# Router logits from unnormalised residual chunks, and modulated rows made by GpSimd and ScalarE, in a four-layer float32 model on one core

## The chip, the core and the metric

The kernel runs on one core of one Trainium2 chip. The metric is the device time of one execution in microseconds (us); less is better. A profiled execution lists every instruction of the five engines: TensorE (PE, and PEld for its weight loads), VectorE (DVE), ScalarE (ACT), GpSimd (POOL) and SyncE (SP, whose DMA queue is SPq), with the names of the tiles that it writes and reads.

## What is computed

Two blocks of two layers each, 512 tokens of width 1024, all float32. The first block has an attention layer and a state-space layer, each followed by a hierarchical mixture of experts (MoE) with 32 experts of which each token takes two. The second block has two layers with a context of 256 tokens beside the 512. The change touches the way into the two MoE layers:

```python
x = x + gate1[:, None, :] * mix
h2 = modulate(rmsnorm(x, norm2_w[layer]), shift2, scale2)   # h * (1 + scale) + shift
# hier_moe(h2, ...), t = h2 by tokens:
g_prob = softmax(t @ w_group + b_group);  g_val, g_idx = top_k(g_prob, 1)
e_logits = einsum('td,dge->tge', t, w_expert) + b_expert     # those of group g_idx
e_val, e_idx = top_k(softmax(e_logits), 2);  e_val = e_val / sum(e_val)
hid = silu(t @ w1[e]) * (t @ w3[e]);  y = sum over the two e of weight * (hid @ w2[e])
```

## The kernel before

Each engine has its own program, written out by hand; the order in the file is the order in which the engine works, and semaphores join them. Activations lie transposed: `xT` and `hT` hold 8 slices of 128 channels by 512 tokens (`hT` has 256 context columns behind them). Weights stream through `ring`, eight slots of 128x8x128 (512 KB each), filled by SyncE in the order of use: a slot is requested again when the product that used it is done (`put`, L1526). A product takes eight matmuls of 128 rows each into one of eight PSUM banks; banks go round in the order of the `job(...)` calls, and a job waits until its bank's last user has been copied out (L691 to L717). A float32 matmul is two instructions in the profile.

The stretch in question comes twice, as layer 0 and layer 1 of the first block:

1. The last product of the mixer gives the residual in eight parts (`outA` for layer 0, `out_part`, job `outM`, for layer 1). VectorE adds each to `xT` (`residual`, L2498; L2885 and following for layer 1), ScalarE squares it (`squares`), VectorE adds up the squares (`sum_square`, L2486).
2. Between these products TensorE has parts of the adaptive modulation: a "quad" is four blocks of modulation columns, computed in four parts of four ring slots (`quad_part`, L803), copied by ScalarE (`quad_out`), turned by `quad_turn` (L818) and added to the bias by VectorE (`quad_add`). Quads 4 and 8 are spread over the routing.
3. `norm_sum` (L828) sums the squares over channels with one product, ScalarE takes the root (`inv_root`: Ln, then Exp, into `rstd`).
4. `modulated` (L2324) on VectorE: for each slice `hT = xT * A * rstd` and then `+ shift`, 16 operations.
5. `moe(l)` on TensorE (L880): the route product of `rw` (36 columns: 4 groups and 32 experts) with the eight slices of `hT`; transposes of `hT` to rows of tokens (`token_rows`, jobs `h_tok`), which ScalarE copies and stores to `h_dram` (four stores of 512 KB); then small products that serve VectorE's chain.
6. `route(l)` on VectorE (L2509): logits with bias, group and expert maxima with masks, "picks", prefix sum over tokens, block and lane of each pair, and at its end the token numbers `pair_u`. Most are operations on 128x16 to 128x200.
7. GpSimd gathers rows of `h_dram` by `pair_u` with indirect DMAs once all rows are stored (`h_rows_stored`), TensorE transposes them (`rows_T`, L961), and the expert steps follow (`up`, L976; `down`, L995).

In layer 1 TensorE also works off three columns of the next block's context product in this stretch (`first_ctx`, `ctx_column`, L876), each 3.6 us, cut in halves between the small products; ScalarE copies them into `ctx_kept`.

GpSimd does nothing else in the stretch. In the state-space stage it forms sums of weights for halved products (`pair_sums`, L3379), four tensor_tensor of 128x512 a pair.

## Time and profile before

| | us |
|---|---|
| median of 3 runs | 3356.8 |
| lowest, highest | 3356.3, 3364.9 |
| profiled execution, its own time | 3363.0 |
| its span, from the first to the last instruction | 3361.0 |

| engine | busy us | share of the span |
|---|---|---|
| TensorE, matmuls | 3218.6 | 96% |
| TensorE, weight loads | 2058.4 | 61% |
| VectorE | 1757.3 | 52% |
| ScalarE | 883.7 | 26% |
| GpSimd | 285.8 | 9% |

The mean granted TensorE clock is 0.982 of full speed, the DMA moved 399 MB. In a timeline each row is a run of like instructions: its start, its length, engine, line of the file, operation, what it writes and reads, how many; in brackets how long the engine was idle before it, and what ended that. The last residual product of layer 0 ends at 294.8 us from the span's start, that of layer 1 at 1056.2.

### The profile page before, as it was taken

How to read it: one execution, taken by the hardware profiler on the slowest of the kernel's cores; microseconds unless marked ns; L12 is line 12 of the kernel's file. 1: busy time of each engine (PE TensorE's matmuls, PEld its weight loads, DVE VectorE, ACT ScalarE, POOL GpSimd, SP SyncE). 2: the span in 40 equal slices, each digit the busy share in tenths (PEclk: the TensorE clock that was granted, in tenths of full speed). 3: DMA queues.
4: the chain of work that ended last, by engine and by line, in shares of the span. 5: the costliest groups of instructions: out<-in, count | busy, mean ns of one | idle time of the engine just before them, and what ended most of it. 6: DMA issues, size and time to landing. Idle time of an engine off the chain costs nothing.

```text
span 3361.0 us, 36905 instructions
## 1 busy us (share of the span) xinstructions
PE 3218.6 (96%) x13516; PEld 2058.4 (61%) x13516; DVE 1757.3 (52%) x3507; ACT 883.7 (26%) x1775; POOL 285.8 (9%) x246
## 2 busy tenths in 40 slices
PE   7988998999999999999999999999999999999998
PEld 4743653777744655565555555555544666878887
DVE  2253235787724236986344454444468854454555
ACT  2241221334321221154232131111111623222212
POOL 1200431243200330000000000000000000000000
PEclk9999999999999899999999999999999999999999
DMA  8646877533247786111111112222222111223232
GB/s 269 215 157 224 312 293 242 161 106 98 82 167 262 288 319 174 31 32 55 38 38 50 51 49 64 57 57 57 58 69 69 37 51 50 76 69 88 82 88 63
DMA packets 427392, 399.00 MB, mean 119 GB/s; under 512 B 28080, under 2 KB 362416, under 8 KB 419792
## 3 DMA queue, kind: packets, MB, share of 16 engines
q1 hardware_dynamic: 393520, 352.60, 33.3%
q10 hardware_dynamic: 15264, 24.07, 2.2%
q0 software_dynamic: 18432, 19.98, 1.8%
q8 instruction: 111, 1.82, 0.2%
q14 instruction: 65, 0.53, 0.1%
HBM read 445.37 MB, written 31.92 MB: 142 GB/s over the span
## 4 chain that ended last, share of the span: by engine, by line
PE 60%; DVE 7%; DMA 2%; issue 1%; ACT 1%; POOL 0%; SPq 0%; DVEq 0%; ACTq 0%; POOLq 0%
PE psum L751 39%; PE psum L736 5%; PE psum L1279 3%; DVE arena L2240 3%; PE psum L976 3%; DMA ring<-in_w_branch 1%; PE psum L995 1%; PE psum L1441 1%; PE psum L1453 1%; PE psum L1365 1%; PE psum L1405 1%; PE psum L1395 1%; DVE arena L2237 1%; PE psum L961 1%; ACT scratch L1662 1%
## 5 line engine op out<-in xcount | busy, mean ns | idle before, releaser
L751 PE MATMUL psum<-arena,ring 128*128 128x384 f32 (+1 forms) x2592 | 747.2, 439 | 13.1 <-DVE psum L2237 6.1
L751 PEld LDWEIGHTS psum<-arena,ring 128*128 128x128 f32 x2592 | 491.9, 191 | 239.8 <-DVE psum L2237 13.3
L751 PE MATMUL psum<-hT,ring 128*128 128x384 f32 (+1 forms) x2176 | 622.1, 439 | 0.0
L751 PEld LDWEIGHTS psum<-hT,ring 128*128 128x128 f32 x2176 | 413.7, 190 | 187.4 <-issue 5.7
L1670 ACT ACTIVATE scratch<-psum 128x256 f32<-128x256 f32 (+1 forms) x411 | 176.2, 429 | 962.4 <-PE psum L751 814.6
L2237 DVE TENSOR_TENSOR ring<-ring 128x512 f32<-128x512 f32 (+1 forms) x336 | 216.1, 662 | 261.8 <-PE psum L751 250.2
L2237 DVE TENSOR_TENSOR psum<-psum,scratch 128x256 f32<-128x256 f32 (+1 forms) x328 | 155.8, 480 | 371.3 <-PE psum L751 270.0
L1670 ACT ACTIVATE arena<-psum 128x512 f32<-128x512 f32 (+5 forms) x414 | 194.2, 500 | 470.3 <-PE psum L736 139.9
L736 PE MATMUL psum<-hT,ring 128*128 128x512 f32 (+1 forms) x704 | 282.5, 562 | 6.0 <-DVE hT L2233 6.0
L1662 ACT ACTIVATE arena<-psum,cols 128x256 f32<-128x256 f32 (+3 forms) x280 | 131.7, 493 | 521.7 <-PE psum L976 228.4
L2240 DVE SCALAR_TENSOR_TENSOR arena<-arena,vec 128x783 f32<-128x783 f32 (+1 forms) x256 | 228.7, 894 | 9.1
L736 PEld LDWEIGHTS psum<-hT,ring 128*128 128x128 f32 x704 | 134.7, 192 | 151.7 <-issue 142.5
L2237 DVE TENSOR_TENSOR arena<-arena 128x512 f32<-128x512 f32 (+13 forms) x252 | 186.3, 753 | 45.4 <-DMA arena<-y_dram 20.9
L2240 DVE SCALAR_TENSOR_TENSOR arena<-arena,psum 128x384 f32<-128x384 f32 (+3 forms) x236 | 98.3, 448 | 206.1 <-ACT arena L1662 195.6
L1064 PE MATMUL psum<-hT,ring 128*128 128x256 f32 x672 | 154.4, 381 | 0.0
L1662 ACT ACTIVATE arena<-arena,cols 128x512 f32<-128x512 f32 (+10 forms) x171 | 137.1, 830 | 54.6 <-DVE arena L2240 24.5
L1064 PEld LDWEIGHTS psum<-hT,ring 128*128 128x128 f32 x672 | 126.4, 190 | 19.8 <-issue 3.4
L2237 DVE TENSOR_TENSOR arena<-psum,scratch 128x384 f32<-128x384 f32 (+1 forms) x80 | 40.8, 510 | 157.1 <-PE psum L751 157.1
L751 PE MATMUL psum<-arena,scratch 128*128 128x384 f32 (+1 forms) x384 | 113.9, 432 | 3.8 <-DVE arena L2237 3.8
L1279 PE MATMUL psum<-arena,ring 128*128 128x512 f32 x256 | 111.8, 595 | 0.9 <-DVE hT L2240 0.9
L976 PE MATMUL psum<-arena 128*64 128x256 f32 x960 | 111.3, 386 | 1.4 <-issue 1.4
L1064 PE MATMUL psum<-arena 128*128 128x256 f32 x448 | 101.3, 379 | 0.0
(269 smaller groups left out, 3605.2 us busy)
## 6 DMA issues: line engine op xcount, KB each, us to landing
ring<-in_w_in SPq DMA_DIRECT2D x177, 512.0 KB, 4.0
arena<-in_moe_w SPq DMA_DIRECT2D x44, 1536.0 KB, 10.9
ring<-in_ada_w SPq DMA_DIRECT2D x96, 512.0 KB, 5.9
ring<-in_w_mod SPq DMA_DIRECT2D x48, 512.0 KB, 5.9
ring<-in_ssm_w_in SPq DMA_DIRECT2D x48, 512.0 KB, 5.5
ring<-in_w_branch SPq DMA_DIRECT2D x64, 256.0 KB, 3.2
hT<-in_moe_w SPq DMA_DIRECT2D x10, 1536.0 KB
ring<-in_moe_w SPq DMA_DIRECT2D x10, 1024.0 KB
```

Source lines behind the costliest of these rows:

```text
L736: mm = nc.tensor.matmul(b[:, 0:n], ws[k // 8][0][:, k % 8, :], rhs(k)[:, o:o + n], start=(k == 0), stop=(k == nk - 1))
L751: mm = nc.tensor.matmul(flat(bank_, nb), lhs[:, k, :], rhs(k), start=(start and k == 0), stop=(k == kd_ - 1), skip_group_check=True)
L961: mm = nc.tensor.transpose(b[:, j * P:(j + 1) * P], rows[:, i % DEEP, k * P:(k + 1) * P], C("ident"))
L976: mm = nc.tensor.matmul(b[LANES * h:LANES * h + LANES, 0:2 * P], rowsT[:, i % 2, k, LANES * h:LANES * h + LANES], step_weights(s, h, 2 * P ...
L995: mm = nc.tensor.matmul(b[LANES * h:LANES * h + LANES, :], hidT[:, i % 2, LANES * h:LANES * h + LANES], step_weights(s, h, w0, S), start=T ...
L1064: mm = nc.tensor.matmul(bank_[:, 0:S // 2], lhs[:, k, :], rhs(k), start=(start and k == 0), stop=(k == 3), skip_group_check=True)
L1279: mm = nc.tensor.matmul(b, ws[k // 8][0][:, k % 8, :], yT[:, k, :], start=(k == 0), stop=(k == 15))
L1365: mm = nc.tensor.matmul(b[:, 0:w], z_w[c][0][:, k, :], hT[:, k, o:o + w], start=(k == 0), stop=(k == KD - 1))
L1662: return nc.scalar.activation(out_, in_, f, bias=bias, scale=scale, **kw)
L1670: return nc.scalar.activation(out_, in_, ACT.Copy)
L2237: return v.tensor_tensor(out_, in0, in1, op)
L2240: return v.scalar_tensor_tensor(out_, in0, s, in1, op0, op1)
```

## The change

Route logits. With A = norm2_w * (1 + scale) the route product of the modulated rows is the root of a token times the product of `rw` with `xT * A`, plus the product of `rw` with the shift. So:

- VectorE writes `hT = xT * A` for each slice as soon as the slice's residual is there (`scaled`), and no longer runs `modulated` ahead of the routing.
- TensorE runs the route product on these: slices 0 to 5 ahead of the last residual product (layer 0) or in its middle (layer 1), slice 6 and slice 7 behind it, on either side of the norm sum (`route_part`). Eight one-column products give the shift's part of the logits (`route_shift`), which VectorE adds to the router's bias.
- VectorE multiplies the product by the root and adds the bias, two operations instead of one.
- GpSimd multiplies the eight slices of `hT` by the root, in place, once the route product has read them; ScalarE adds the shift. Both run beside VectorE's routing chain.
- Token rows are transposed by halves (channels 0 to 511 of all tokens, then the rest), placed among the small products; ScalarE stores each half by itself, eight stores of 256 KB.
- Parts 2 and 3 of quads 4 and 8 come behind the logits' transposes. In layer 1 the context columns are no longer cut in halves, quad 5 moves one residual product earlier, and its turn ahead of the last one; the context's modulation on VectorE moves from c = 6 to c = 5.

```diff
+            def route_part(l, k0, k1):
+                if k0 == 0:
+                    eng.wait_ge(rw_landed, pe.at(("rw", l)))
+                    b, full = job("route_shift", l)
+                    eng.wait_ge(vector_done, pe.at(("quad", (1, 4)[l])))
+                    for k in range(KD):
+                        mm = nc.tensor.matmul(b[0:36, 0:1], rw[:, k, :], col("mod", 48 * l + 24 + k), start=(k == 0), stop=(k == KD - 1))
...
+                for k in range(k0, k1):
+                    eng.wait_ge(vector_done, pe.at(("scaled", l, k)))
+                    mm = nc.tensor.matmul(b[0:36, :], rw[:, k, :], hT[:, k, 0:S], start=(k == 0), stop=(k == KD - 1))
...
             def moe(l):
+                route_part(l, KD - 2, KD - 1)
+                quad_part(QUAD_MOE[l], 0)
+                norm_sum(f"n2_{l}")
+                route_part(l, KD - 1, KD)
                 quad_part(QUAD_MOE[l], 1)
...
@@ TensorE, layer 0
                 linear(("outA", c), lambda k: aT[:, k, :])
                 if c == 6:
                     quad_turn(3)
+                    if stage_on(2):
+                        route_part(0, 0, KD - 2)
...
@@ TensorE, layer 1
-                    if c >= 4:
-                        quad_part(5, c - 4)
-                    out_part(c, 0, 16)
+                    if c < 7:
+                        quad_part(5, c - 3)
+                        out_part(c, 0, 16)
                 quad_turn(5)
+                out_part(7, 0, 8)
+                if stage_on(4):
+                    route_part(1, 0, KD - 2)
+                out_part(7, 8, 16)
...
@@ ScalarE, moe
+                for half in range(2):
+                    for k in range(4 * half, 4 * half + 4):
+                        eng.wait_ge(gpsimd_done, ac.at(("rooted", l, k)))
+                        act(hT[:, k, 0:S], hT[:, k, 0:S], ACT.Identity, bias=col("mod", 48 * l + 24 + k)).then_inc(scalar_done, ac.step(("h", f"n2_{l}", k)))
+                    if half == 0:
+                        quad_out(QUAD_MOE[l])
+                for half in range(2):
+                    for t in range(4):
                         evac(("h_tok", l, t, half), h_tok[:, t, half * S:(half + 1) * S])
-                    if t == 0:
-                        quad_out(QUAD_MOE[l])
-                    eng.wait_ge(scalar_done, ac.own())
-                    eng.dma_start(h_dram[l][t * P:(t + 1) * P, :], h_tok[:, t, :]).then_inc(h_rows_stored, 16)
+                        eng.wait_ge(scalar_done, ac.own())
+                        eng.dma_start(h_dram[l][t * P:(t + 1) * P, half * S:(half + 1) * S], h_tok[:, t, half * S:(half + 1) * S]).then_inc(h_rows_stored, 16)
+                    if l and half == 0:
+                        evac(("att_k", 0, 0, "c"), ctx_kept[:, 0:L], n=L, name=("ctx_kept", 0))
...
@@ VectorE
+            def scaled(l, k):
+                eng.wait_ge(vector_done, ve.own())
+                ts(hT[:, k, 0:S], xT[:, k, :], col("A", k)).then_inc(vector_done, ve.step(("scaled", l, k)))
...
             def route(l):
+                eng.wait_ge(rb_landed, ve.at(("rb", l)))
+                b, free = full("route_shift", l)
+                tt(rb[0:36, :], rb[0:36, :], b[0:36, 0:1], ALU.add).then_inc(vector_done, ve.step(free))
                 b, free = full("route", l)
-                eng.wait_ge(rb_landed, ve.at(("rb", l)))
-                ts(logitT[0:36, :], b[0:36, :], rb[0:36, :], op0=ALU.add).then_inc(vector_done, ve.step([free, ("biased", l)]))
+                eng.wait_ge(scalar_done, ve.at(("rstd", f"n2_{l}", "x")))
+                tt(logitT[0:36, :], b[0:36, :], rstd[0:36, 0:S], ALU.mult).then_inc(vector_done, ve.step([free, ("rstd_used", f"n2_{l}")]))
+                eng.wait_ge(vector_done, ve.own())
+                ts(logitT[0:36, :], logitT[0:36, :], rb[0:36, :], op0=ALU.add).then_inc(vector_done, ve.step(("biased", l)))
...
-                modulated("n2_0", V("norm2_w", 0, 8), M(0, 4, 0, 8), lambda k: M(0, 3, k), lambda k: xT[:, k, :])
...
@@ GpSimd, moe
-                eng.wait_ge(h_rows_stored, 64 * (l + 1))
+                eng.wait_ge(tensor_done, po.at(("full",) + jobname("route", l)))
+                eng.wait_ge(scalar_done, po.at(("rstd", f"n2_{l}", "x")))
+                for k in range(KD):
+                    g_.tensor_tensor(hT[:, k, 0:S], hT[:, k, 0:S], rstd[:, 0:S], ALU.mult).then_inc(gpsimd_done, po.step(("rooted", l, k)))
+                eng.wait_ge(h_rows_stored, 128 * (l + 1))
```

TensorE around the last residual product of layer 0 (L736), up to the second weight part of quad 4, in the order before. L814 is a weight part, L834 the norm sum, L886 the route product.

```order
L736 MATMUL psum<-arena,ring 128x512 x7
L814 MATMUL psum<-ring,arena 32x512 [waits weights_1,weights_2,weights_0,weights_3,vector_done]
L814 MATMUL psum<-ring,arena 32x512 x7
L834 MATMUL psum<-scratch,ones 128x512 [waits vector_done]
L814 MATMUL psum<-ring,arena 32x512 [waits weights_6,weights_7,weights_5,weights_4]
L814 MATMUL psum<-ring,arena 32x512 x7
L886 MATMUL psum<-hT,arena 36x512 [waits vector_done,rw]
L886 MATMUL psum<-hT,arena 36x512 [waits vector_done] x7
```

The same place in the order now; L889 is the shift's product, L895 the route product, L918 the logits' transposes.

```order
L889 MATMUL psum<-cols,arena 36x1 x7
L895 MATMUL psum<-hT,arena 36x512 [waits vector_done] x6
L736 MATMUL psum<-arena,ring 128x512 [waits vector_done,weights_7]
L736 MATMUL psum<-arena,ring 128x512 x7
L895 MATMUL psum<-hT,arena 36x512 [waits vector_done]
L814 MATMUL psum<-ring,arena 32x512 [waits weights_1,weights_2,weights_0,weights_3,vector_done]
L814 MATMUL psum<-ring,arena 32x512 x7
L834 MATMUL psum<-scratch,ones 128x512 [waits vector_done]
L895 MATMUL psum<-hT,arena 36x512 [waits vector_done]
L814 MATMUL psum<-ring,arena 32x512 [waits weights_6,weights_7,weights_5,weights_4]
L814 MATMUL psum<-ring,arena 32x512 x7
L918 MATMUL psum<-const,arena 128x36 [waits vector_done]
```

Six slices of the route product and the shift's product have moved ahead of the last residual product; one slice stands on each side of the norm sum, and the logits' transposes follow the second weight part.

TensorE in layer 1, from the third context column to the row transposes, before. L876 is a context column; of the small products that serve VectorE's chain L938 is for the experts, L944 for the pairs, L951 for the weights of the slots; L961 are the row transposes.

```order
L876 MATMUL psum<-hT,arena 128x256 [waits scalar_done,vector_done,ctx_w]
L876 MATMUL psum<-hT,arena 128x256 x3
L938 MATMUL psum<-arena,ones 128x16 [waits vector_done,scalar_done]
L944 MATMUL psum<-arena 128x24 [waits vector_done,scalar_done]
L944 MATMUL psum<-arena 128x24 x7
L876 MATMUL psum<-hT,arena 128x256 x4
L951 MATMUL psum<-arena 128x24 [waits vector_done]
L951 MATMUL psum<-arena 128x24 x7
L961 MATMUL psum<-const,arena 128x128 [waits scalar_done,rows_0]
```

The same place now, from the last token rows (L912) and the turn (L824) on; L957 is for the experts, L963 for the pairs, L970 for the weights of the slots, and the row transposes follow.

```order
L912 MATMUL psum<-const,hT 128x128 [waits scalar_done] x8
L824 MATMUL psum<-const,arena 128x8 [waits scalar_done]
L824 MATMUL psum<-const,arena 128x8 x3
L876 MATMUL psum<-hT,arena 128x256 [waits scalar_done,vector_done,ctx_w]
L876 MATMUL psum<-hT,arena 128x256 x7
L957 MATMUL psum<-arena,ones 128x16 [waits vector_done]
L963 MATMUL psum<-arena 128x24 [waits vector_done,scalar_done]
L963 MATMUL psum<-arena 128x24 x7
L876 MATMUL psum<-hT,arena 128x256 [waits scalar_done,vector_done,ctx_w]
L876 MATMUL psum<-hT,arena 128x256 x7
L970 MATMUL psum<-arena 128x24 [waits vector_done]
L970 MATMUL psum<-arena 128x24 x7
```

Token rows stand among the small products, and two whole context columns stand between the turn and the weights of the slots, where two halves of one column stood.

## Rows read from the trace of the kernel before

**Rows 1.** Busy time by stretch (us, engines' busy us and instructions, clock, DMA).
```profile
296.00:345.00 49.00, 34.12 (x180) 20.47 (x174) 26.78 (x94) 10.43 (x19) 6.12 (x6) 0.77 0.64 225
1056.00:1106.00 50.00, 45.73 (x240) 28.62 (x239) 27.93 (x96) 11.20 (x20) 6.02 (x6) 0.88 0.71 248
```
**Rows 2.** TensorE's timeline, layer 0, 270 to 350 us.
```profile
287.68 7.11 PE L736 MATMUL psum<-arena,ring 128*128 128x512 f32 x16
294.72 1.92 PE L814 MATMUL psum<-ring,arena 128*32 128x512 f32 x16
297.32 1.10 PE L834 MATMUL psum<-scratch,ones 128*128 128x512 f32 x2 [0.67 <-DVE cols L2237]
...
302.02 8.16 PE L886 MATMUL psum<-hT,arena 128*36 128x512 f32 x16 [1.55 <-DVE hT L2233]
...
314.71 0.44 PE L902 MATMUL psum<-const,arena 36*128 36x36 f32 x4
...
321.81 0.60 PE L919 MATMUL psum<-const,arena 128*32 128x128 f32 x4 [3.90 <-DVE arena L2237]
...
341.15 3.65 PE L961 MATMUL psum<-const,arena 128*128 128x128 f32 x16
```
**Rows 3.** TensorE's timeline, layer 1, 1000 to 1125 us.
```profile
1042.38 13.97 PE L1279 MATMUL psum<-arena,ring 128*128 128x512 f32 x32 [0.86 <-DVE hT L2240]
1056.19 0.95 PE L824 MATMUL psum<-const,arena 128*128 128x4 f32 x8
...
1061.72 1.92 PE L814 MATMUL psum<-ring,arena 128*32 128x512 f32 x16 [1.68 <-DMA ring<-in_w_mod]
...
1072.77 3.64 PE L814 MATMUL psum<-ring,arena 128*32 128x512 f32 x32
...
1079.38 3.62 PE L876 MATMUL psum<-hT,arena 128*128 128x256 f32 x16
...
1095.58 3.76 PE L876 MATMUL psum<-hT,arena 128*128 128x256 f32 x8
...
1102.41 1.95 PE L961 MATMUL psum<-const,arena 128*128 128x128 f32 x8
```
**Rows 4.** VectorE's timeline, layer 0, 270 to 350 us.
```profile
315.18 0.31 DVE L2515 COPY arena<-psum 128x144 f32<-128x144 f32 x1 [4.22 <-PE psum L902]
...
317.30 0.78 DVE L2243 TENSOR_REDUCE arena<-arena 128x8 f32<-128x32 f32 x5
...
321.71 0.48 DVE L2570 MEMSET arena<- 32x512 f32 x1
...
335.84 0.18 DVE L2623 CAST pair_u<-arena 128x24 uint32<-128x24 f32 x1
```
**Rows 5.** VectorE's timeline in the state-space stage, 640 to 690 us.
```profile
660.92 0.42 DVE L2237 TENSOR_TENSOR psum<-psum,scratch 128x256 f32<-128x256 f32 x1
...
680.72 1.38 DVE L2237 TENSOR_TENSOR arena<-arena,hT 128x512 f32<-128x512 f32 x1
```
**Rows 6.** GpSimd's timeline in the same stretch.
```profile
660.85 1.27 POOL L3394 TENSOR_TENSOR arena<-ring,arena 128x512 f32<-128x512 f32 x1
...
680.29 1.27 POOL L3392 TENSOR_TENSOR arena<-arena,ring 128x512 f32<-128x512 f32 x1
```
**Rows 7.** ScalarE's timeline, layer 0, 270 to 350 us.
```profile
299.24 0.72 ACT L1662 ACTIVATE scratch<-scratch,cols 128x512 f32<-128x512 f32 x1
...
317.44 1.08 ACT L1670 ACTIVATE arena<-psum 128x512 f32<-128x512 f32 x2 [0.42 <-PE psum L893]
...
318.93 1.09 ACT L1670 ACTIVATE arena<-psum 128x512 f32<-128x512 f32 x2 [0.40 <-ACT arena L1670]
```
**Rows 8.** TensorE by stretch: us, busy, clock, DMA share, GB/s; layer 1.
```profile
1064.00:1068.00 4.00, 3.97 (x9) 1.00 1.02 367
```
**Rows 9.** The same view, two stretches of one us in layer 0.
```profile
322.00:323.00 1.00, 0.41 (x4) 0.71 1.01 408
346.00:347.00 1.00, 1.00 (x10) 0.84 1.02 430
```

More of the change, by code:

```diff
@@ L903, in moe @@
                 mm.then_inc(tensor_done, pe.step(full))
-                for t in range(1, 4):
-                    token_rows(t)
+                quad_part(QUAD_MOE[l], 2)
+                quad_part(QUAD_MOE[l], 3)
                 def first_ctx(i, k0, k1):
@@ L2889, in _ @@
                     if c == 6:
+                        quad_add(5)
+                        eng.wait_ge(vector_done, ve.own())
+                        stt(col("A", 0, 8), M(1, 4, 0, 8), 1.0, V("norm2_w", 8, 8), ALU.add, ALU.mult).then_inc(vector_done, ve.step())
+                        for k in range(KD - 1):
+                            scaled(1, k)
+                    if c == 7:
+                        scaled(1, 7)
+                    if c == 5:
                         stt(col("A2", 0, 8), col("mod2", 32, 8), 1.0, V("norm_w_2", 0, 8), ALU.add, ALU.mult).then_inc(vector_done, ve.step())
```

66 lines of the change are left out of this document (30 added, 36 removed).

## The prediction

> **What bounds the kernel now.** I read the busy time by stage first. TensorE is busy for 96% of the span, and the two routing stages are among the few places where it is not: 34.1 of 49 us in the first mixture-of-experts layer (layer 0), 45.7 of 50 us in the second (layer 1) [rows 1]. Second, TensorE's timeline in both. In layer 0 the last residual product ends at 294.8 and the first transposes of gathered rows start at 341.15, so routing takes 46.3 us; TensorE waits 1.55 us for the modulated rows, 3.9 us for the picks, and several times behind them [rows 2]. In layer 1 the same stretch runs from 1056.2 (where the turn that follows that product starts) to 1102.4, 46.2 us, but context columns fill it, such as the one that starts at 1079.38, and the waits sum to about 4 us (50.0 less 45.7, [rows 1]), 1.68 of it a wait for streamed weights [rows 3]. Third, VectorE's timeline: a chain of short operations on 128 partitions, logits copied at 315.18, picks done when the memset of 321.71 starts (6.5 us), token numbers cast at 335.84, which frees the gathers [rows 4]. What bounds layer 0 is that chain; layer 1 is bound by TensorE's own work almost as much as by the chain.
>
> **The change, part by part.** I call the end of the last residual product T before and T' after, and count from it.
>
> *Ahead of T'.* Six of eight slices of the route product now run ahead of the last residual product (layer 0) or in its middle (layer 1). A 512-column product of one slice costs 7.1/8 = 0.89 us [rows 2], so 5.3 us. They were in the routing stretch before, where the eight took 8.2 us, paced by VectorE. New are eight one-column products for the shift. Where the trace has none like them, the nearest are those of the turn: narrow instructions cost 0.95/8 = 0.12 us each however narrow [rows 3]; at two instructions a product that is 1.9 us at most; at nothing, 0. I take 1.7. TensorE has no idle time ahead of T, so nothing covers this: T' is 7.0 us later than T. In layer 1 the turn (0.95) also moves ahead of T', and the wait of 0.86 us at the last residual product [rows 3] should go, since that product's weights are now requested earlier: 7.1 us.
>
> *The root off the chain.* After T' come slice seven 0.9, the first weight part 1.9, the norm sum 1.1, slice eight 0.9: the route product is full at 4.8. The root is ready 1.5 us after the norm sum (which ends at 298.4 [rows 2], the Exp at 299.96 [rows 7]), at 5.4. The multiply by the root takes 0.75, like the biased copy before, then the new bias add 0.4, the logits' transposes 0.45 [rows 2]: logits copied at about 8, where it was 20.35 before (315.18 less 294.83). VectorE's 16 operations of modulation leave this path, and the two weight parts (2 and 3) that stood ahead of the logits' transposes now stand behind. That is a lead of 12 us for the chain. The eight added scaling operations hide under TensorE's 7 us products; were they late, slices one to six would be.
>
> *GpSimd beside the chain.* Eight products 128x512 of two SBUF inputs start at 5.5 and take 1.27 each, as GpSimd's weight sums do [rows 6]. That is where the lead is spent. The trace shows it in the state-space stage. GpSimd's product at 680.29 ends at 681.56; VectorE's two-input operation of 512 columns that started at 680.72 took 1.38 and ended at 682.10, half a microsecond after GpSimd's, so most of what it took was waiting. The tensor_tensor at 660.92, which reads PSUM and one SBUF tile, took 0.42 beside GpSimd's product of 660.85 and waited for nothing [rows 5, 6]. So a two-input operation of VectorE waits for the GpSimd product under way to end. Of the routing chain nearly every tensor_tensor has two SBUF inputs; the reductions and the PSUM reads have one. While GpSimd has products left, the chain gets about one such operation per 1.3 to 1.4 us. GpSimd is done at 5.5 + 8 x 1.27 + 8 x 0.2 for VectorE's turns = 17.3. By then about ten operations of the chain are through (bias add, group maximum, group pick, the four masks) and what starts at 317.30 in the old trace (4.4 us to the picks [rows 4]) is left: picks at 21.7. If the four masks pass together it is 20.5. I take 21.6. Before, it was 26.9. The rule of the Trainium skill, page "SBUF — State Buffer", section "Who interferes with whom", says the same: a VectorE instruction with two SBUF inputs contends with a GpSimd instruction that reads SBUF, and whoever is second fully blocks. It speaks against this change, and the row at 680.72 agrees. By it the picks come at 21.6; with no such hold they would come at 14.4, which is rival A.
>
> *Streamed weights.* After T' ten transfers of 512 KB are still to come (two of part 1, parts 2 and 3), since a ring of eight slots can only be refilled as it is used. The DMA moved 367 GB/s there [rows 8]: 5.24 MB in 14.3 us plus a microsecond to start. Part 3 lands at 15 and is used by 17. Before, parts 2 and 3 were used at 16.5 and later (1072.77, [rows 3]) and never waited; now TensorE reaches them at 8 and waits 2.1 and 3.7 us. In layer 0 that hides behind the chain (17 against 21.6).
>
> *Layer 0 after the picks.* The chain behind the picks is as it was, 19.4 us to the row transposes with its waits (321.71 to 341.15 [rows 2, 4]); TensorE has the token transposes between the steps now, at the half clock, which costs 0.6. Row transposes at 21.6 + 19.4 + 0.6 = 41.6 instead of 46.3: -4.7, with +7.0 ahead of T': **+2.3 us**.
>
> *Layer 1 after the picks.* TensorE has more to do here: eight token groups (3.8 us), ctx column 1 and 2 whole (3.6 each [rows 3]). The second-half token transpose needs the bank of context column 0, which ScalarE empties only behind four copies and four stores of the first half; two copies and a store take 1.5 us (317.44 to 318.93 [rows 7]), so a copy and a store 1.05 by estimate, and so that bank is free at 27. Slots go at 28 instead of 27, the pair product starts at 34.2 (the chain alone would have it 1.5 us earlier), gathers are issued at 38.5, and TensorE is through column 2 and the weight product between 43.5 (full clock) and 47.7 (half clock; the eight slices at 1095.58 took 3.76 at it [rows 3]). I take 45.3 against 46.2: -0.9, with +7.1: **+6.2 us**.
>
> Expert loads start when part 3 is used, 3 us later than before against a first use 22 us on; nothing there. The last row store goes out at about 30 (31 in layer 1), 3 us to land, and token numbers come at 36 (38); were the copies 3 us later, this store would end the wait. The sum is 2.3 + 6.2 = 8.5 us. The profiled execution took 3363.0 (span 3361.0), the median of the runs is 3356.8; I put the sum on the median: **3365 us**, 0.25% slower, inside what a measurement of this kernel can tell from no change (0.3%, 10 us).
>
> **Rivals.**
> *A, VectorE is not held.* For it: no row shows operations of 0.17 us beside GpSimd; four masks without waits may slip through together with their followers. Against: [rows 5, 6]. Picks at 14.4; TensorE ends part 3 at 17 and is next: picks transposed at 17.1 in layer 0 (26.98 before), -9.9 + 7.0 = -2.9; in layer 1 column 0 ends at 20.9, 0.7 earlier than in my forecast, +5.5. Sum +2.6, 3359.
> *B, the clock holds and faster.* The granted clock fell to half between 322 and 323 in layer 0, behind the wait for the picks, and came back between 346 and 347 [rows 9]. With fewer idle microseconds it could stay up. The column slices of 1095.58 would take 1.8 instead of 3.76, the sixteen transposes of 341.15 half of their 3.65 [rows 2, 3], and their neighbours likewise: by estimate 4 us in each layer. On top of A: -6, 3351. Against: the sparse stretch behind the picks is still there.
> *C, an early clock fall, slower.* The idle time before the picks was 3.9 us when the clock fell [rows 2, 9]. Now TensorE is busy 1.9 of the 7.2 us from 7.8 to 15 while it waits for weights. If the clock falls there, part 3 costs 3.8 instead of 1.9 and column 0 up to 7.2 instead of 3.6, until the clock comes back (dense work ran from 341.15 at the latest to past 346 before it did [rows 2, 9], by estimate 5 to 9 us): in layer 1 the picks are transposed at 25.3, not 21.7, +3.7; together +12 to +13, 3370. In layer 0 the chain hides it. It decides if the fall comes before 16.
> *D, the change does not do what it says*: the logits come no earlier, because slice eight or the root is late. Both have producers that were there before; 2%, inside the range.
>
> **How the numbers follow.** Forecast 0.50 (+3 to +12), A 0.22 (0 to +5), B 0.08 (-10 to -3), C 0.18 (+9 to +18), D 0.02. The range takes B's near half to C's upper end: 3351 to 3375. Faster by over 0.3% needs both layers at their best: 0.05. Slower by over 0.3% is three quarters of C and a quarter of the forecast: 0.26. Same: 0.69.
>
> **What would show it.** Right: T' 7 us later; logits copied near 8; two-input operations of VectorE of 1 to 1.4 us between them and GpSimd's last product; waits of TensorE for weights ahead of parts 2 and 3; picks at 20 to 22; the row transposes of layer 1 no earlier than 43 after T'. Wrong: VectorE's chain still at 6.5 us beside GpSimd; shift products of next to nothing; a gain of over 5 us in layer 1, which would mean that its idle time was larger than its 4 us, or that its clock stayed up.

## The result, and the profile after it

| | before | changed |
|---|---|---|
| median of 6 runs (lowest to highest) | 3357.8 us (3355.1 to 3364.9) | 3375.2 us (3371.0 to 3378.2) |
| profiled execution: time, span | 3363.0, 3361.0 | 3375.5, 3373.6 |

The ratio is 1.0044, 95% interval 1.0033 to 1.0054: slower by 0.44%, some 15 us. The forecast was 3365 (3351 to 3375). The measured median lies at the upper edge of the range, 0.2 us past it; the ratio, put on the median of 3356.8 that the forecast started from, gives 3371.6, inside it. The prediction gave 0.69 to a change of at most 0.3% and 0.26 to a loss of more than that, and it was the loss.

Busy time by stretch in the changed kernel (columns as in [rows 1]; the first two answer to those rows, the third is in the attention stage of the first layer, ahead of all that was changed):

```profile
304.00:349.00 45.00, 30.33 (x169) 18.08 (x168) 26.45 (x80) 15.10 (x24) 14.30 (x13) 0.72 0.68 230
1075.00:1125.00 50.00, 38.07 (x219) 23.62 (x219) 26.52 (x81) 16.74 (x28) 16.08 (x14) 0.83 0.72 245
168.00:190.00 22.00, 17.05 (x54) 9.89 (x54) 14.54 (x41) 8.90 (x28) 0.00 (x0) 0.62 0.62 224
```

TensorE is busy for 38.1 us of layer 1's routing stretch, where it was 45.7 of as many. The third row explains a part of the difference that is not the change's: the granted clock in 168 to 190 us was 0.62, in the profiled execution of before 0.84, and the last residual product of layer 0 ended 9.8 us later, of which the inserted work is only 5.9. So I compare stretches from T', not times of day.

TensorE's timeline of the changed kernel, layer 0 (answers to [rows 2]; columns: start us, duration us, engine, line, operation, output<-inputs, shapes, count, idle time before it and what ended it):

```profile
290.81 0.95 PE L824 MATMUL psum<-const,arena 128*128 128x4 f32 x8
291.70 0.72 PE L889 MATMUL psum<-cols,arena 128*36 128x1 f32 x16
292.28 5.32 PE L895 MATMUL psum<-hT,arena 128*36 128x512 f32 x12
297.53 7.13 PE L736 MATMUL psum<-arena,ring 128*128 128x512 f32 x16
304.59 1.05 PE L895 MATMUL psum<-hT,arena 128*36 128x512 f32 x2
...
312.19 0.41 PE L918 MATMUL psum<-const,arena 36*128 36x36 f32 x4 [0.55 <-DVE arena L2260]
315.60 2.74 PE L814 MATMUL psum<-ring,arena 128*32 128x512 f32 x16 [3.00 <-DMA ring<-in_ada_w]
321.51 3.64 PE L814 MATMUL psum<-ring,arena 128*32 128x512 f32 x16 [3.17 <-DMA ring<-in_ada_w]
...
325.99 1.01 PE L937 MATMUL psum<-const,arena 128*32 128x128 f32 x4
...
347.09 3.25 PE L980 MATMUL psum<-const,arena 128*128 128x128 f32 x14 [1.41 <-DMA arena<-h_dram,pair_u]
```

T' is 304.6. The insert takes 5.9 us: from the start of the turn (290.81) to the start of the last residual product (297.53) it is 6.7 us, before it was 0.8 (286.87 to 287.68). Part 2 waits 3.00 and part 3 3.17 us for their weights; part 3 ends at 325.1, 20.5 after T'. Rows are transposed 42.5 after T' (before: 46.4 after T).

VectorE and GpSimd beside it (the routing chain, answers to [rows 4]):

```profile
312.63 0.31 DVE L2552 COPY arena<-psum 128x144 f32<-128x144 f32 x1 [0.59 <-PE psum L918]
312.98 0.17 DVE L2270 TENSOR_REDUCE arena<-arena 128x4 f32<-128x16 f32 x1
313.18 1.26 DVE L2264 TENSOR_TENSOR arena<-arena 128x16 f32<-128x16 f32 x1
314.47 1.19 DVE L2260 TENSOR_SCALAR arena<-arena 128x16 f32<-128x16 f32 x1
315.69 1.22 DVE L2264 TENSOR_TENSOR arena<-arena,const 128x16 f32<-128x16 f32 x1
316.94 0.17 DVE L2270 TENSOR_REDUCE arena<-arena 128x4 f32<-128x16 f32 x1
317.15 3.65 DVE L2264 TENSOR_TENSOR arena<-arena 128x16 f32<-128x16 f32 x5
...
325.23 0.48 DVE L2607 MEMSET arena<- 32x512 f32 x1
```
```profile
310.49 10.05 POOL L3404 TENSOR_TENSOR hT<-hT,scratch 128x512 f32<-128x512 f32 x8 [161.82 <-ACT scratch L1683]
343.54 1.19 POOL L3377 DMA_INDIRECT arena<-h_dram,pair_u  x1 [22.99 <-DMA h_dram<-arena]
```

The logits are copied 8.0 after T'. Until GpSimd is done at 320.5, operations of 0.17 us with tiles in SBUF take 1.2 (reductions excepted), and the five of 317.15, of which the first is the group mask, 3.65 (0.71 before). The picks are there at 325.2, 20.6 after T', after a chain of 12.6 us (6.5 before). The gather of 343.54 was ended by the row stores, not by the token numbers (cast at 340.2).

Layer 1, first its weights at the third output product, some 90 us ahead of T', where the change multiplies quad 5 one product earlier; then the head of the routing (answers to [rows 3]):

```profile
970.41 11.32 PE L1298 MATMUL psum<-arena,ring 128*128 128x512 f32 x26
983.88 1.92 PE L814 MATMUL psum<-ring,arena 128*32 128x512 f32 x16 [2.15 <-DMA ring<-in_ada_w]
988.11 15.67 PE L1298 MATMUL psum<-arena,ring 128*128 128x512 f32 x32 [2.31 <-DMA ring<-in_ssm_w_out]
```
```profile
1068.11 7.13 PE L1298 MATMUL psum<-arena,ring 128*128 128x512 f32 x16
1075.17 1.05 PE L895 MATMUL psum<-hT,arena 128*36 128x512 f32 x2
...
1082.78 0.41 PE L918 MATMUL psum<-const,arena 36*128 36x36 f32 x4 [0.33 <-DVE arena L2260]
1086.64 3.64 PE L814 MATMUL psum<-ring,arena 128*32 128x512 f32 x16 [3.46 <-DMA ring<-in_w_mod]
1092.70 3.64 PE L814 MATMUL psum<-ring,arena 128*32 128x512 f32 x16 [2.42 <-DMA ring<-in_w_mod]
1096.27 4.67 PE L876 MATMUL psum<-hT,arena 128*128 128x256 f32 x16
1100.78 0.60 PE L937 MATMUL psum<-const,arena 128*32 128x128 f32 x4
```

And the granted clock (the last column but two) in stretches of it:

```profile
1080.00:1084.00 4.00, 2.70 (x21) 0.82 (x20) 2.27 (x5) 1.83 (x4) 2.93 (x3) 1.00 1.01 367
1084.00:1088.00 4.00, 1.36 (x8) 0.45 (x12) 3.86 (x5) 1.96 (x3) 4.00 (x4) 0.57 1.02 361
1092.00:1096.00 4.00, 3.30 (x16) 0.68 (x16) 3.54 (x22) 0.00 (x0) 0.00 (x0) 0.50 0.00 1
1100.00:1120.00 20.00, 17.60 (x121) 15.56 (x119) 9.80 (x36) 6.31 (x13) 2.68 (x3) 1.00 0.69 240
```

T' is 1075.2. TensorE idled 3.5 us from 1083.2 on, the clock went to its lower level (0.50), and parts 2 and 3 took 3.64 each instead of 1.9. The picks were transposed 25.6 after T', though they had been made at 20.6.

### The profile page after: what moved, and what is told of

It reads as the page before. It is cut to its first block, busy times and chain, and to the rows that moved or that the text cites. A ratio compares the mean times of both kernels' runs of the same rounds, so it can differ in the third digit from the quotient of the medians.

```text
span 3373.6 us, 37016 instructions
## 1 busy us (share of the span) xinstructions
PE 3221.9 (96%) x13548; PEld 2056.5 (61%) x13548; DVE 1763.1 (52%) x3495; ACT 895.3 (27%) x1791; POOL 305.5 (9%) x262
## 4 chain that ended last, share of the span: by engine, by line
PE 81%; DVE 7%; DMA 3%; ACT 2%; issue 2%; ACTq 0%; POOL 0%; SPq 0%; DVEq 0%; POOLq 0%
PE psum L751 39%; PE psum L1083 7%; PE psum L736 7%; PE psum L995 5%; PE psum L1298 3%; DVE arena L2267 3%; PE psum L1014 3%; DMA ring<-in_w_branch 1%; PE psum L980 1%; PE psum L1462 1%; PE psum L1474 1%; PE psum L1261 1%; PE psum L814 1%; PE psum L1386 1%; PE psum L843 1%
## 5 line engine op out<-in xcount | busy, mean ns | idle before, releaser
L736 PE MATMUL psum<-hT,ring 128*128 128x512 f32 (+1 forms) x704 | 281.1, 559 | 5.8 <-DVE hT L2260 5.8
L736 PEld LDWEIGHTS psum<-hT,ring 128*128 128x128 f32 x704 | 134.2, 192 | 150.9 <-issue 142.1
L2264 DVE TENSOR_TENSOR arena<-arena 128x512 f32<-128x512 f32 (+13 forms) x252 | 195.5, 790 | 44.9 <-DMA arena<-y_dram 20.4
L2264 DVE TENSOR_TENSOR arena<-psum,scratch 128x384 f32<-128x384 f32 (+2 forms) x82 | 42.2, 514 | 163.1 <-PE psum L751 157.4
L2267 DVE SCALAR_TENSOR_TENSOR xT<-psum,cols,xT 128x512 f32<-128x512 f32 (+1 forms) x64 | 37.7, 613 | 122.5 <-PE psum L736 62.2
```

Of the source, the lines that this page charges most:

```text
L736: mm = nc.tensor.matmul(b[:, 0:n], ws[k // 8][0][:, k % 8, :], rhs(k)[:, o:o + n], start=(k == 0), stop=(k == nk - 1))
L2264: return v.tensor_tensor(out_, in0, in1, op)
L2267: return v.scalar_tensor_tensor(out_, in0, s, in1, op0, op1)
```

## The experiments

Twelve kernels in four batches (numbers 1 to 4, 5 to 8, 9 and 10, 11 and 12); each batch with runs of the kernel before beside it (medians 3361.2, 3360.5, 3360.6 and 3359.0 us).

**1. Quad 5 alone.** Before, with only quad 5 multiplied and loaded one product earlier:

```diff
-                    if c >= 4:
-                        quad_part(5, c - 4)
+                    if c < 7:
+                        quad_part(5, c - 3)
```

> The kernel before with one thing of the change only: quad 5 is read and multiplied one residual product earlier (c = 3 to 6 instead of 4 to 7), its turn and its bias stay where they were. Theory (the stall is in the prefetch): in the changed kernel TensorE waits 2.15 us for the first weight part of quad 5 and 2.31 us for the residual product behind it, and that product takes 15.7 instead of 14.0 us, 6.1 us in all, and the 0.86 us wait at the last residual product is gone; so +4 to +6 us. Rival (the stall belongs to the new order of DMAs and banks elsewhere in the changed kernel): +0 to +1 us.

Measured: 3365.1, ratio 1.0012 (1.0003 to 1.0021).

```profile
966.53 11.32 PE L1279 MATMUL psum<-arena,ring 128*128 128x512 f32 x26
979.98 2.81 PE L814 MATMUL psum<-ring,arena 128*32 128x512 f32 x16 [2.13 <-DMA ring<-in_ada_w]
984.28 15.67 PE L1279 MATMUL psum<-arena,ring 128*128 128x512 f32 x32 [1.50 <-DMA ring<-in_ssm_w_out]
```

Before, TensorE goes through here without a wait. From the code I read it so: products 0 to 2 keep their slots until their last slices are multiplied together, and four more loads of 512 KB come into an interval in which hardly a slot is free. The 0.86 us wait that the move removes costs two waits of 3.6 us together, a part at 2.81 instead of 1.92 and a product at 15.67 instead of 14.00. From the first of these products to T it is 97.8 us, 5.4 more than before.

**2 and 3. The change in one layer.** In layer 0 alone (the layer 1 code as before, quad 5 too), and in layer 1 alone with quad 5:

```diff
-                route_part(l, KD - 2, KD - 1)
-                ...
+                if l in NEW:
+                    route_part(l, KD - 2, KD - 1)
+                    ...
+                else:
+                    ...
```

> The change in layer 0 only; layer 1 as before, quad 5 too. Theory (the sum of the terms of the prediction, with the shift's products at 0.7): T' 6.0 later, 42.4 from T' to the row transposes instead of 46.3: +2 us. Rival (GpSimd's hold costs more than the lead in each layer): +5 or more. Other rival (layer 0 gains by itself, the whole loss is in layer 1): -3 or less.

> The change in layer 1 only, with quad 5 one product earlier; layer 0 as before. Theory: +6 to +7 from slices, shift and turn ahead of T' with nothing gained behind it (45.8 instead of 46.2 us to the row transposes), and +5 from the prefetch stall: +11 to +13 us. Rival (clock falls and noise of the attention stage make up a third of the measured +17): +7 or less.

Measured: layer 0 alone 3362.5, ratio 1.0002 (0.9991 to 1.0013); layer 1 alone 3376.6, ratio 1.0039 (1.0024 to 1.0054). Together they make 1.0041 of the 1.0044. The loss is layer 1's: about 13 us, of which quad 5 alone is 4.

**4. GpSimd's products cut to one column.** The change, with the hold on VectorE taken away by making its cause small:

```diff
-  g_.tensor_tensor(hT[:, k, 0:S], hT[:, k, 0:S], rstd[:, 0:S], ALU.mult)
+  g_.tensor_tensor(hT[:, k, 0:1], hT[:, k, 0:1], rstd[:, 0:1], ALU.mult)
```

> The changed kernel with GpSimd's eight products cut to one column each, so the rows that the experts get are not multiplied by the root. Theory (VectorE waits for GpSimd's product under way): the chain from the copied logits to the picks goes from 12.6 us (312.63 to 325.23) back to 6.5 us in both layers; TensorE is then held by the weight parts 2 and 3, so the row transposes come 3 to 4 us earlier in layer 0 and 0 to 1 us in layer 1: 3 to 5 us less than the changed kernel, still +11 to +14 against before. Rival (the chain is slow for another reason, such as ScalarE or the semaphores of eight more steps): chain above 11 us, no gain.

Measured: 3375.5, ratio 1.0042 (1.0029 to 1.0056), the same as the change. The chain is back at 6.5 us (logits copied at 312.46, picks at 318.98), so the hold was real, 6.1 us in each layer. And it was worth nothing, where I had expected 3 to 5 us. TensorE, layer 0 of this kernel:

```profile
316.29 3.31 PE L814 MATMUL psum<-ring,arena 128*32 128x512 f32 x16 [3.86 <-DMA ring<-in_ada_w]
322.40 2.60 PE L814 MATMUL psum<-ring,arena 128*32 128x512 f32 x16 [2.80 <-DMA ring<-in_ada_w]
...
325.84 1.06 PE L937 MATMUL psum<-const,arena 128*32 128x128 f32 x4
```

Picks made at 319 are transposed at 325.8, behind part 3. In layer 1 they are transposed 22.5 after T' instead of 25.6, and yet the rows come at 46.2 (45.75 in the change).

**5. The slices behind T'.** The change with its insert taken away from before T' in both layers, quad 5 back in its place:

```diff
-                    if stage_on(2):
-                        route_part(0, 0, KD - 2)
...
-                route_part(l, KD - 2, KD - 1)
-                quad_part(QUAD_MOE[l], 0)
+                route_part(l, 0, 2)
                 norm_sum(f"n2_{l}")
-                route_part(l, KD - 1, KD)
-                quad_part(QUAD_MOE[l], 1)
+                route_part(l, 2, KD)
+                quad_part(QUAD_MOE[l], 0)
...
+                quad_part(QUAD_MOE[l], 1)
                 quad_part(QUAD_MOE[l], 2)
...
```

Part 1 now stands behind the logits' transposes. The turn of quad 5 stays in the middle of the last product.

> The changed kernel, with what it put ahead of the last residual T' taken away again: the shift product and slices 0 to 5 stand behind T' in both layers (order now: shift, slices 0 and 1, the norm's sum, slices 2 to 7, quad part 0, logits, parts 1 to 3), and layer 1's quad 5 is multiplied where it was before the change, only its turn stands in the middle of the last output product. GpSimd's products stay as they are. Theory (the change loses by what it puts on TensorE and on the weights' path ahead of T', 6.0 us in layer 0 and about 10 in layer 1, and gains less behind it): T' comes back to its place of before, the 2.1 and 2.3 us waits for quad 5's and the output weights go, logits are copied about 12.5 after T' instead of 8, picks at about 25 with the hold (12.6 us of chain), rows transposed about 43 to 44.5 after T' against 46.3 and 46.2 before: 2 to 3 us less than before the change in each layer, total 3352 to 3358 beside 3357 to 3361 before, against 3375 for the change. Rival (layer 1 loses by something else in its head, the clock fall or the ctx columns): T' of layer 1 comes back but the stretch behind it stays at 46 or more, total 3360 to 3366.

**6. The same with GpSimd's products split** around the picks, each also waiting for its own slice of the route product only:

```diff
-  eng.wait_ge(tensor_done, po.at(("full",) + jobname("route", l)))
   ...
   for k in range(KD):
+      if k == 4:
+          eng.wait_ge(vector_done, po.at(("picks", l)))
+      eng.wait_ge(tensor_done, po.at(("routed", l, k)))
```

> As the run with the slices behind T', and GpSimd's eight products are split: product k waits for route slice k and the root alone, so that 0 to 3 can start some 5 us before the route product ends, and 4 to 7 wait until the picks are made. Theory (the hold of 6 us on VectorE's two-input operations is real, and it was worth nothing in the changed kernel only because weight parts 2 and 3 stand ahead of the transposed picks there; with the slices behind T' the weights are in by 17 and used by about 21 and bind no more): chain of the routing from logits copied to picks back to about 6.5 us, picks about 19 to 20 after T', picks transposed at 21 to 22, rows transposed at 39 to 42, total 4 to 6 us per layer under the kernel before, 3347 to 3352. Rival 1 (the hold is worth nothing anywhere): the same time as the run with the slices behind T', within 2 us. Rival 2 (the row stores take over, since h 4 to 7 now come about 8 us later): the gather ends its wait by the row stores, and rows are transposed at 43 or later: no gain over the other run or a loss.

Measured: 3375.3, ratio 1.0041 (1.0027 to 1.0054), and 3371.9, ratio 1.0048 (1.0031 to 1.0065). Both theories of mine missed by 17 us and more. Number 6, layer 0:

```profile
304.14 1.92 PE L814 MATMUL psum<-ring,arena 128*32 128x512 f32 x16
306.00 0.43 PE L916 MATMUL psum<-const,arena 36*128 36x36 f32 x4
306.36 1.92 PE L814 MATMUL psum<-ring,arena 128*32 128x512 f32 x16
314.25 3.64 PE L814 MATMUL psum<-ring,arena 128*32 128x512 f32 x16 [5.97 <-DMA ring<-in_ada_w]
319.59 3.29 PE L814 MATMUL psum<-ring,arena 128*32 128x512 f32 x16 [1.70 <-DMA ring<-in_ada_w]
```
```profile
300.00:304.00 4.00, 4.00 (x10) 0.90 (x8) 0.00 (x0) 1.92 (x3) 3.45 (x3) 1.00 0.01 2
308.00:312.00 4.00, 0.28 (x4) 0.00 (x0) 3.52 (x24) 0.00 (x0) 0.00 (x0) 1.00 1.00 374
```

T' is back at 294.7, as before, and the picks are made 18.3 after it. But I had moved parts 0 and 1 behind the product, and the DMA engines stand still meanwhile (2 GB/s at 300 to 304): it is part 0 that gives free the slots for the loads of part 2. From the end of part 0 (306.1) to the start of part 2 it is 8.2 us; in the change it is 8.1 (307.5 to 315.6), in number 5 8.3. Picks are transposed 28.7 and 28.6 after T' in the two kernels, and 31.9 and 30.3 in layer 1; before 27.1 and 27.3. The rows come 50.4 and 50.1 after T' in layer 0, 55.4 and 53.9 in layer 1 (before 46.4 and 46.2): 13 and 11 us together, about what the two kernels lose. What lies between picks and rows grew too; in layer 1 the context column there took 5.64 and 5.42 us instead of 3.70 in the change. The weights do not land "at 17 after T'"; they land so long after part 0 was multiplied.

**7 and 8. Part 3 behind the product for the ends,** and with it all token rows of half 0, quad_out behind all biases; then the same with the one-column products:

```diff
-                quad_part(QUAD_MOE[l], 3)
...
                 b, full = job("ends", l)
...
+                quad_part(QUAD_MOE[l], 3)
+                token_rows(0, 0, 1, 2, 3)
```

> The changed kernel with two things moved: on TensorE quad part 3 stands behind the product for the ends (and with it all token rows of half 0), so that the transposes of the picks wait for weight part 2 only; on ScalarE quad_out stands behind the biases of h 4 to 7. Both restraints that stood beside GpSimd's hold are so lifted, the hold is left. Theory (hold and weights are two restraints of the same length, and each hides the other): picks stay at 20.6 after T' in both layers, the picks' transposes start within 0.3 us of them (1.0 later in layer 0 and up to 3 in layer 1 before this edit), a gain of 0 to 2 us a layer, partly paid back by the token rows that now come later; total 3370 to 3376 beside 3375 for the change. Rival (weights alone bind, the hold never does): picks are early enough and the total falls by 4 us or more, to 3371 or less.

> As the run with quad part 3 and quad_out moved, and GpSimd's eight products cut to one column each, which leaves the rows of tokens 1 to 511 without the root. It differs from that run by the hold alone, as the run with one-column products differed from the change (0.0 us there). Theory (two restraints of one length): now the hold is worth something: picks about 15 after T' instead of 20.6, transposed at once (part 2 ends about 14 to 17 after T'), 2 to 5 us less per layer than the run with full products, total 3362 to 3371. Rival (weights alone, or the row stores, bind the head whatever the hold): within 2 us of the run with full products, as in the pair before.

Measured: 3386.8, ratio 1.0077 (1.0057 to 1.0096), and 3374.4, ratio 1.0044 (1.0026 to 1.0061). The first is 11 us worse than the theory allowed: the picks were transposed as they came (at 326.08), but part 3 and the token rows, 7.1 us of work, then stood ahead of the transposes for the slots, which I had not priced. The pair answers the question nevertheless: the hold, worth 0 between the change and number 4, is worth 12.4 us in the median between these two. They have only four runs each, but every run of number 8 (3371.8 to 3378.5) is faster than every one of number 7 (3380.3 to 3389.7). In the profiles 9.3 of it lies between T' and the rows: 7.0 in layer 0, 49.4 to 42.4, and 2.3 in layer 1. With part 3 ahead of the picks, hold and weights run side by side and end together (20.6 and 20.5 after T'), and to take away the hold alone gains nothing. That taking away the wait for the weights alone would gain nothing either is argued and not shown, for number 7 changed more than that wait.

**9 and 10. Parts 0 and 1 first.** Slices behind T', part 0 at once behind T', part 1 behind the norm's sum (shown against numbers 5 and 6); number 9 with split products and the token rows of half 1 behind the slots, number 10 with all eight products as their slices and the root come:

```diff
+                quad_part(QUAD_MOE[l], 0)
                 route_part(l, 0, 2)
                 norm_sum(f"n2_{l}")
+                quad_part(QUAD_MOE[l], 1)
                 route_part(l, 2, KD)
-                quad_part(QUAD_MOE[l], 0)
...
-                quad_part(QUAD_MOE[l], 1)
...
```

> The run with the slices behind T' and GpSimd's products split, with quad part 0 back to the first place behind T' and part 1 behind the norm's sum, ahead of slices 2 to 7 (in the run before they stood behind the route product and behind the logits, and ended 11.3 and 13.6 after T' in layer 0); and the token rows of half 1 behind the product for the slots, with ScalarE's copies of half 0 ahead of the biases of half 1. Theory (what binds the head is when parts 0 and 1 are multiplied, since their ring slots are what parts 2 and 3 are loaded into: 8.2 us from the end of part 0 to the landing of part 2 and 5.3 more for part 3 in that run): part 0 ends at 1.9 and part 1 at about 7.5 after T', part 2 lands at about 10 and part 3 at 16, both used by 20 to 22; the route product ends 1.7 later than without them, picks at about 21.5, transposed at 22 to 23 in layer 0 (before the change 27.1), rows transposed at 41 to 43 (46.4): 3 to 5 us less than before the change per layer, total 3349 to 3355. Rival (the picks come as early, but the row stores, moved back by the late half of the rows, take over): the gather's wait ends by the row stores and the rows are transposed at 45 or later, total 3358 to 3364.

> As the run with parts 0 and 1 early, but GpSimd's products are not split (each waits for its own slice and the root alone), and token rows and ScalarE's order stay as in the change. Theory: GpSimd runs from about 7.5 to 18 after T', so that it holds VectorE for 3 us of a chain that starts at 15: picks at about 23, h complete at 18.5, stores early; rows transposed at 42.5 to 44, total 3351 to 3358, between the kernel before and the run with split products. Rival (the row stores decide in the split run): this run is the faster of the two by 1 to 3 us.

Measured: 3364.7, ratio 1.0008 (0.9999 to 1.0017), and 3357.8, ratio 0.9991 (0.9981 to 1.0000). Number 9 is 7 us below number 6, number 10 17 us below number 5, the largest difference of the study. Neither pair differs in parts 0 and 1 alone (number 9 also has the later token rows, number 10 the earlier start of GpSimd), so how much of it is theirs is not separated. Number 10, layer 0:

```profile
300.29 1.92 PE L814 MATMUL psum<-ring,arena 128*32 128x512 f32 x16
...
315.44 1.92 PE L814 MATMUL psum<-ring,arena 128*32 128x512 f32 x16
318.10 1.92 PE L814 MATMUL psum<-ring,arena 128*32 128x512 f32 x16 [0.74 <-DMA ring<-in_ada_w]
...
323.27 0.60 PE L936 MATMUL psum<-const,arena 128*32 128x128 f32 x4 [2.66 <-DVE arena L2260]
...
342.61 3.31 PE L979 MATMUL psum<-const,arena 128*128 128x128 f32 x16
```

Part 2 waits for nothing, part 3 for 0.74, both run at the full clock, and rows are transposed 42.3 after T' (46.4 before): 4.1 gained in layer 0. In layer 1 nothing is gained: 46.2, and the gather waits for the row stores there.

```profile
1098.76 1.07 POOL L3373 DMA_INDIRECT arena<-h_dram,pair_u  x1 [23.70 <-DMA h_dram<-arena]
```

Number 9 came out in the range of its rival, but not by its mechanism alone. In layer 0 its gather is ended by the row stores, and rows are still transposed 43.2 after T'. In layer 1, where they come at 48.6, the token numbers end the gather's wait; ahead of them TensorE stands before the token rows of half 1 until ScalarE has added the shift (1089.9 to 1091.1).

**11 and 12. The row stores.** Number 10 with the token rows of half 0 ahead of the picks and quad_out behind the biases; then also the load of expert 5 behind the stores:

```diff
-                        eng.wait_ge(tensor_done, sp.at(("full",) + jobname("h_tok", l, 3, 1)))
+                        eng.wait_ge(h_rows_stored, 128 * (l + 1))
```

> As the run with unsplit products and early parts 0 and 1, with the token rows of half 0 transposed ahead of the picks (layer 1's first ctx column halved around them) and ScalarE's quad_out behind all eight biases: ScalarE then copies and stores rows from about 20.5 after T' instead of 22.8 in layer 0 and 24.5 in layer 1, and TensorE does the transposes in a gap of 2.7 us in layer 0. Theory (layer 1's gather waited 2.3 us for the last row store, issued at 32.4 after T' and landed 8 us later beside an expert's load of 1.5 MB; layer 0's did not wait): stores issued 2 to 3 us earlier, layer 1's rows transposed 1 to 3 us earlier (44 to 45 after T' instead of 46.2), layer 0's unchanged within 0.5, total 1 to 3 us less than that run, 3353 to 3357 beside 3358 to 3361 before. Rival (the expert's load is issued by the last of these transposes and moves with them, so that the stores wait for it as before): no gain in layer 1, the total within 1 us of that run.

> As the run with the rows first, and the load of expert 5 (1.5 MB into hT) waits for the row stores instead of the last transposed token rows. Theory (the load shares the DMA engines with the last stores and makes them land 6 to 8 us after their issue): the stores land within 3 to 4 us of their issue, the gather in layer 1 starts with the cast of the row numbers, and rows are transposed at 42 to 43.5 after T'; 1 to 2 us less than the run with the rows first. Rival (the load, pushed back, now shares the engines with the gathered rows instead, or is late for its own step): the gather starts earlier and its rows land later, total the same or up to 3 us more.

Measured: 3356.7, ratio 0.9993 (0.9984 to 1.0002), and 3355.4, ratio 0.9992 (0.9983 to 1.0001). Number 11 transposes layer 1's rows 44.3 after T'. In number 12 the gather is no longer ended by the stores:

```profile
1098.57 1.07 POOL L3372 DMA_INDIRECT arena<-h_dram,pair_u  x1 [24.93 <-DVE arena L2259]
```

The stores themselves came sooner: in layer 1 the slowest landed 4.2 us after its issue, in number 11 8.4. But the gather comes no earlier, and rows are transposed 46.5 after T', where I had expected 42 to 43.5. Parts 2 and 3 took 5.3 us there (3.8 in layer 0) at a granted clock of 0.72 (1072 to 1078), and from the transposed picks to the cast of the token numbers it was 17.0 us, 14.8 in number 10. That stretch grew because the clock was lower in it too: 0.65 in 1088 to 1095, where number 11 has 1.00, with the context column at 5.58 instead of 3.70. The medians of numbers 10 to 12 lie 2 to 4 us under that of the kernel before, within what can be told from no change. They do not beat it by a measurable amount.

## Why the prediction was right or wrong

**The insert ahead of T'**: forecast 7.0, measured 5.9. The slices are right (5.3); sixteen one-column instructions took 0.72, not 1.7.

**The step that failed: "the wait of 0.86 us at the last residual product should go".** It went. But the sum has nothing for what the same move costs. I priced the move of quad 5 at the place where it pays and not where its loads now fall, 90 us earlier: 4.5 us of waits, and a product at 15.67 instead of 14.00 with the clock at 0.62 behind them. That is +6.1 - 0.9 = +5.2 instead of -0.9. Number 1 shows it alone: +5.4 ahead of T in its profile, +4 us in the median. My text says that a ring of eight slots can only be refilled as it is used, and did not apply it here.

**Root off the chain, logits at 8**: 8.0 in both layers. Luck had a part in this: the terms that I listed add up to 7.0, and the bias add, forecast at 0.4, took 0.88 beside GpSimd's first product.

**GpSimd's hold**: picks forecast at 21.6, measured at 20.6 in both; the chain grew from 6.5 to 12.6. The term "8 x 0.2 for VectorE's turns" was wrong: GpSimd lost hardly anything to VectorE: its eight products took 10.05 us together (four took 4.96 in number 6, where VectorE was idle) and ended 15.9 after T', not 17.3. I had also counted two-input operations alone, but VectorE's tensor_scalar operations, with one tile and a column or a constant, were held too (314.47, 1.19 us for 16 columns). The rule of the Trainium skill ("SBUF — State Buffer", section "Who interferes with whom") holds for both: the section lists tensor_scalar among the operations that can contend with GpSimd, beside those with two SBUF inputs.

**Streamed weights**: part 3 was forecast to land at 15 and to be used by 17; it started at 16.9 and ended at 20.5 in layer 0, since the clock had halved in the waits (0.57 in 316 to 320). I wrote that this "hides behind the chain (17 against 21.6)". It hid, but with the margin gone: it was level with the chain. This made rival A's price wrong: without the hold, -5.9 us against the forecast; numbers 4 and the change give 0.0.

**Layer 0**: +2.3 forecast; the profile gives +5.9 - 3.9 = +2.0, and alone it cannot be told from 0. This is the right sum out of terms that were partly off (insert 1.1 less, row stores about 2 more: ScalarE's quad_out waits for part 3 ahead of the biases of h 4 to 7, so the last store is issued at 336.8 and not 30 after T'). I had named that end ("were the copies 3 us later, this store would end the wait").

**Layer 1**: +6.2 forecast, about +13 by the ratio of number 3. The profile places it. Before, the output products that follow the state-space stage start here:

```profile
963.80 25.05 PE L1279 MATMUL psum<-arena,ring 128*128 128x512 f32 x58
```

From there to T (1056.2) it is 92.4 us, and in the change from 970.41 to T' (1075.2) 104.8. So 12.4 us are lost ahead of T', where the sum had 7.1: insert 1.1 less, quad 5's loads 6.1 more. Behind T' it is 45.75 against 46.2, -0.5 where the sum had -0.9. In the profile of number 3 the two are +10.8 and +2.6.

Rival C, which I gave 0.18, had the mechanism behind T': TensorE idle at 1083, clock halved until past 1096, parts 2 and 3 at 3.64, the context column at 4.67, picks transposed at 25.6 (C said 25.3). But its price of 3.7 us is not in this profile: the half clock of before behind the picks (0.50 at 1094 to 1106) is at full level now, which gives it back. Number 4 says the same, with picks 3 us earlier and rows no earlier. In number 3, with the same late picks, 2.6 us stayed. So C's total of 3370 was nearer to the measured one than mine largely by luck: the loss is in the weights of quad 5, ahead of T', which C did not have either.

**What it all hung on.** The head of the routing has three restraints of nearly the same length: VectorE's chain with the hold, the parts of the quad, the row stores. The change took 12 us off the way to the logits, of which the hold took 6 back, and set that chain beside two others, one of which it had itself moved back: part 0 stands behind a slice now, 1.0 us after a T' that is 5.9 us later, and so do all loads that follow it. Numbers 4 to 8 find another restraint behind the one that they move. With chain and weights moved (number 10) layer 0 gains 4.1 us in the profile, with the row stores too (number 11) the layers gain 4 and 2; in number 12 the 2 are gone again with the clock. None of this is a measurable gain in the total.

## What to carry to other kernels

Where streamed weights pass through a ring, look for the instruction that frees the slots: in this kernel it set the pace for all later ones. Try it first, and price any move of a weight product at the place where its loads now fall. Before pricing the removal of a wait, write down when each of the other things that the next instruction needs is there; if a second is within a few microseconds, removing the first is worth that margin and no more. Price a wait also by what it may do to the clock behind it, and read the clock's rows in both kernels. An experiment that removes a suspected cost and shows no gain does not clear it: take away the second restraint and ask again.

## What the hardware showed that was not expected

- GpSimd's back-to-back products of 512 columns (1.26 us each) hold VectorE's small operations to one per product, and lose hardly any time themselves (eight in 10.05): 16 columns took 1.19 to 1.26 us instead of 0.17, tensor_scalar like tensor_tensor; reductions (0.17) and copies from PSUM (0.31) went through. In number 10 a tensor_scalar of 36x512 took 1.41 beside GpSimd, in number 9 0.48 without it.
- Sixteen one-column matmul instructions took 0.72 us together, 0.045 each.
- In the change's layer 1 TensorE stood idle from 1083.2 to 1086.6, and the granted clock went from 1.00 (1080 to 1084) to 0.57 (1084 to 1088); it was at 1.00 again in 1100 to 1120, behind the context column and dense transposes. In number 10 no part waited over 0.9 us and the clock stayed at 1.00 from 1050 to 1102, although TensorE had stood idle for 2.3 us ahead of the logits' transposes. In number 12, with the same 2.3 us and no wait behind them, it was 0.72 from 1072 to 1078. So a wait in mid-work can cost twice; what decides whether it does, these runs do not show.
- With a load of 1.5 MB issued in the middle of the row stores the slowest store of 256 KB in layer 1 landed 8.4 us after its issue (number 11), with the load behind them 4.2 (number 12).
